# A down projection rewritten from a plain product into seven block products

## The reference, cut to what matters

```python
h = rmsnorm(x, g_norm2) * (1.0 + sc2) + sh2
x = x + gt2 * ((silu(h @ w_gate) * (h @ w_up)) @ w_down)   # w_down: 5632 x 2048, fp32
return rmsnorm(x, g_final)                                 # x: 512 tokens x 2048
```

## Time and profile before

| | |
|---|---|
| median of three runs | 2304.39 us |
| span of the profiled execution, first to last instruction | 2303.3 us |
| TensorE busy in the span | 2249.0 us (98%) |
| VectorE busy | 1532.3 us (67%) |
| ScalarE busy | 887.8 us (39%) |
| GpSimd busy | 233.0 us (10%) |
| mean granted TensorE clock | 0.987 |

### The profile page before, as it was taken

One profiled execution on the slowest core, in us unless ns is written; L12 is line 12 of the kernel. 1 busy time (PEld: TensorE's weight loads), 2 busy tenths in 40 slices (PEclk: granted clock), 3 DMA queues, 4 the chain that ended last, 5 costly groups with the idle time before them and its releaser, 6 DMA issues.

```text
span 2303.3 us, 27075 instructions
## 1 busy us (share of the span) xinstructions
PE 2249.0 (98%) x10486; PEld 1866.6 (81%) x10486; DVE 1532.3 (67%) x1734; ACT 887.8 (39%) x1048; POOL 233.0 (10%) x90
## 2 busy tenths in 40 slices
PE   5999999999999999999999999999999999999998
PEld 5878878888877788788888888888888888888887
DVE  5968667474766757677887788778878544444444
ACT  4333232323246222444444444444444433333333
POOL 0002433333420013000000000000000001010001
PEclk7999999999999999999999999999999999999999
DMA  9943444444541777234444445344434845554553
GB/s 362 377 143 114 166 145 148 150 163 161 183 166 37 275 266 263 92 102 146 155 164 137 145 138 173 128 138 163 160 131 148 326 184 203 193 188 183 192 193 128
DMA packets 188198, 404.43 MB, mean 176 GB/s; under 512 B 11328, under 2 KB 67920, under 8 KB 172496
## 3 DMA queue, kind: packets, MB, share of 16 engines
q1 hardware_dynamic: 175088, 387.10, 47.4%
q10 hardware_dynamic: 13024, 16.13, 2.0%
HBM read 383.27 MB, written 19.92 MB: 175 GB/s over the span
## 4 chain that ended last, share of the span: by engine, by line
PE 90%; DVE 4%; issue 2%; ACT 1%; DMA 1%; POOL 1%; SPq 1%; POOLq 0%; DVEq 0%; ACTq 0%
PE ps L1791 27%; PE ps L1793 27%; PE ps L1792 27%; PE ps L1948 1%; DVE acc L1102 1%; DMA araw<-in_w_ada 1%; PE ps L2235 1%; PE ps L1961 1%; PE ps L1959 1%; DVE acc L1339 1%; PE ps L1882 0%; PE ps L1823 0%; PE ps L2060 0%; PE ps L1937 0%; PE ps L1843 0%
## 5 line engine op out<-in xcount | busy, mean ns | idle before, releaser
L931 ACT ACTIVATE whi<-wraw 128x1024 fp32r<-128x1024 f32 x200 | 211.0, 1061 | 276.5 <-DVE wraw L1614 153.3
L1595 DVE TENSOR_TENSOR wlo<-wraw,whi 128x1024 fp32r<-128x1024 f32 x200 | 240.6, 1219 | 76.8 <-ACT whi L931 76.8
L1791 PE MATMUL ps<-d_hi,whi 128*128 128x512 f32 (+1 forms) x736 | 280.1, 381 | 0.0
L1793 PE MATMUL ps<-d_hi,wlo 128*128 128x512 f32 (+1 forms) x736 | 279.6, 380 | 0.0
L1792 PE MATMUL ps<-d_lo,whi 128*128 128x512 f32 (+1 forms) x736 | 279.6, 380 | 0.0
L1791 PE MATMUL ps<-h_hi,whi 128*128 128x512 f32 x680 | 271.6, 399 | 0.0
L1793 PE MATMUL ps<-h_hi,wlo 128*128 128x512 f32 x680 | 267.0, 393 | 0.0
L1792 PE MATMUL ps<-h_lo,whi 128*128 128x512 f32 x680 | 266.5, 392 | 0.0
L1707 DVE TENSOR_TENSOR d_lo<-d_raw,d_hi 128x2048 fp32r<-128x2048 f32 (+1 forms) x44 | 99.7, 2267 | 243.3 <-ACT d_hi L998 243.3
L1791 PE MATMUL ps<-whi,sk_hi 128*128 128x512 f32 x640 | 250.8, 392 | 0.0
L1793 PE MATMUL ps<-whi,sk_lo 128*128 128x512 f32 x640 | 249.4, 390 | 0.0
(11 more groups left out here) (332 smaller groups left out, 3866.3 us busy)
## 6 DMA issues: line engine op xcount, KB each, us to landing
araw<-in_w_ada SPq DMA_DIRECT2D x64, 1024.0 KB, 6.0
wraw<-in_w_gate SPq DMA_DIRECT2D x88, 512.0 KB, 3.9
wraw<-in_w_up SPq DMA_DIRECT2D x88, 512.0 KB, 4.7
d_raw<-aT_keep SPq DMA_DIRECT2D x44, 1024.0 KB, 4.8
wraw<-in_w_down SPq DMA_DIRECT2D x44, 1024.0 KB, 7.1
wraw<-in_w_in SPq DMA_DIRECT2D x38, 1024.0 KB, 5.3
acc<-in_w_up SPq DMA_DIRECT2D x40, 512.0 KB, 5.5
wraw<-in_w_out SPq DMA_DIRECT2D x16, 1024.0 KB, 8.2
```

The source lines that it names most:

```text
L931: A(EHI[e % 4], src, ACT.Copy).then_inc(uhi_ok, 1)
L1595: V_.tensor_tensor(ELO[e % 4], src, EHI[e % 4].bitcast(F32), ALU.subtract).then_inc(ulo_ok, 1)
L1791: pe.matmul(o, w_hi, m_hi, start=first, stop=False)
L1793: return pe.matmul(o, w_lo, m_hi, start=False, stop=last)
```

## The change

The down projection is cut into blocks: tokens into halves of 256 (a1., a2.), each hidden chunk into halves of 256 rows, and output columns into two groups of 1024 (`n` = 0, 1), each halved into 512. Seven block products replace eight:

| product | block of a | block of w_down | when |
|---|---|---|---|
| P1 | a11 | B11 | early |
| P5 | a21-a22 | B11+B12 | early |
| P6 | a21-a22-a11 | B11+B12+B22 | early |
| P4 | a22 | B11+B12+B22+B21 | early |
| P7 | a11-a21 | B12+B22 | late |
| P2 | a12 | B21 | late |
| P3 | a12+(a21-a22-a11) | B22 | late |

A pass over the 11 chunks does the four early products, a second one the three late ones, and that for both groups: 44 steps (`s`), 154 entries. An entry has 12 matmuls of 512 columns, two 128-token tiles t by two k tiles by three. Now the activations are stationary and the weights move, so the result is tokens x columns, and x1 (not the result) is turned on TensorE (`turn_x1`, 16 x 4 transposes in the late steps of n = 0).

- All seven blocks of a are made per chunk in the unit stage (`combine_a`, four VectorE subtractions or additions of 128x512, each waiting for the one before), and stored in `a_keep` (four rows of 512 per chunk become seven; three more stores on ScalarE's queue per unit, `keep_sums`).
- Of w_down, SyncE loads four pieces of 512 KB in an early step and three in a late one, since the pieces are read again in the late pass. VectorE makes three sums in an early step, one in a late step (`down_sum`, L1913).
- ScalarE makes all high parts (`block_hi`, `down_hi`), VectorE all low parts (`block_lo` L1976, `down_lo` L1902). The entries use the ring of four EHI/ELO buffers of the unit stage.
- The gate gt2 becomes a row (`gain_row`, `gtb`), the squares are summed by ScalarE's accumulation, and GpSimd adds no more squares.
- The two halves of tokens at the end are gone; `take`, `join_x1`, `final_mean` and `scaled_out` end the kernel.

```diff
+        def down_order(s):
+            n, late, j = down_step(s)
+            if late:
+                if s < STEPS - 2:
+                    return [(s, "P7"), (s, "P2"), (s, "P3")]
+                return [(s + i, p) for ps_ in (("P7", "P2"), ("P3",)) for i in range(2) for p in ps_] if s == STEPS - 2 else []
+            if s == 0:
+                return [(0, "P1"), (0, "P5"), (0, "P6")]
+            if s == 1:
+                return [(1, "P1"), (1, "P5"), (0, "P4"), (1, "P6"), (1, "P4")]
...
+        def sums_after(e):
+            due = [(s, name, FIRST_E[s] + i - 2 + (s == 2) + (s == STEPS - 1))
+                   for s in range(STEPS) for i, name in enumerate(("P7",) if down_step(s)[1] else ("P5", "P6", "P4"))]
...
 @block.sync
+            def down_loads(s):
+                if s < 2:
+                    sp.wait_ge(ulo_ok, 28 * NU - 3 + 3 * s)
+                else:
+                    sp.wait_ge(ulo_ok, E0 + END_E[s - 2])
+                for i, (rows, col) in enumerate(((lower, far), (upper, far), (upper, near)) if late else
+                                                ((lower, near), (lower, far), (upper, far), (upper, near))):
+                    sp.dma_start(DRAW[s % 2][i]..., w_down[0, rows, col]...).then_inc(dw_ld[s % 2][i], 16)
...
+            for s in range(STEPS):
+                down_loads(s)
+                if s >= 2:
+                    down_blocks(s)
+                if s == 2:
+                    sp.wait_ge(u_used, 28 * NU)
+                    sp.dma_start(gfb[:], gf.partition_broadcast(P)).then_inc(x_ld[0], 16)
+                    x1_piece(0)
+                    x1_piece(1)
+                if s == NCH + 4:
+                    sp.dma_start(gtb[:], gt_keep...partition_broadcast(P)).then_inc(wg_ld, 16)
+                    x1_piece(2)
+                if s == NCH + 6:
+                    x1_piece(3)
...
 @block.scalar
+            def down_hi(e):
+                s, name = DOWN[e]
+                if e < 4:
+                    act.wait_ge(u_used, 28 * NU - 3 + e)
+                else:
+                    act.wait_ge(u_used, E0 + e - 3)
...
 @block.vector
+            def combine_a(u):
+                V_.tensor_tensor(s3, a11, a21, ALU.subtract).then_inc(ac_ok, 1)
+                dve.wait_ge(ac_ok, 4 * u - 3)
+                V_.tensor_tensor(a21, a21, a22, ALU.subtract).then_inc(ac_ok, 1)
+                dve.wait_ge(ac_ok, 4 * u - 2)
+                V_.tensor_tensor(s2, a21, a11, ALU.subtract).then_inc(ac_ok, 1)
+                dve.wait_ge(ac_ok, 4 * u - 1)
+                V_.tensor_tensor(s4, a12, s2, ALU.add).then_inc(ac_ok, 1)
...
+            for e in range(len(DOWN)):
+                if e == 1:
+                    sum_low(NCH)
+                if e == 2:
                     sum_high(NCH)
+                down_lo(e)
+                if e == 2:
                     sum_up(NCH)
+                if e == 3:
                     join_high(NCH)
+                if e == 4:
                     join_low(NCH)
+                if e == 8:
+                    combine_a(NCH)
+                for s, name in sums_after(e):
+                    down_sum(s, name)
...
+                if e == 2:
+                    block_lo(1)
+                for s in range(2, STEPS):
+                    if e == END_E[s - 2] + 4:
+                        block_lo(s)
...
 @block.tensor
+            def down_entry(e):
+                pe.wait_ge(dal_ok, s + 1)
+                pe.wait_ge(ulo_ok, E0 + e + 1)
+                if j == 0:
+                    pe.wait_ge(*{(0, "P1"): (end_ok, 6 * NCH - 10), (0, "P5"): (end_ok, 6 * NCH - 6), ...
+                for t in range(2):
+                    for k in range(2):
+                        last = mm3(ps[bank + t][:], d_hi[s % 2][:, blk, part], d_lo[s % 2][:, blk, part],
+                                   EHI[e % 4][:, c0], ELO[e % 4][:, c0], j == 0 and k == 0, j == NCH - 1 and k == 1)
```

More of the change, by code:

```diff
@@ L504, in _, with chunk_kept @@
[L504 to L509, removed]
+            def chunk_kept(c):
+                sp.wait_ge(at_st[0], 16 * (c + 1))
+                sp.wait_ge(at_st[1], 32 * (c + 1))
+                sp.wait_ge(as_st, 32 * (c + 1))
+            def down_loads(s):
+                n, late, j = down_step(s)
+                lower, upper = slice(j * S, j * S + HT), slice(j * S + HT, j * S + S)
+                near, far = slice(2 * n * S, 2 * n * S + S), slice(2 * n * S + S, 2 * n * S + 2 * S)
+                if s < 2:
[4 more added lines that the diff above has]
+                                                ((lower, near), (lower, far), (upper, far), (upper, near))):
+                    sp.dma_start(DRAW[s % 2][i].rearrange("p (k c) -> p k c", k=2),
+                                 w_down[0, rows, col].rearrange("(k p) c -> p k c", p=P)).then_inc(dw_ld[s % 2][i], 16)
@@ L510, in _ @@
+            for n, tb in enumerate((2, 3, 0, 1)):
+                for half in range(2):
+                    sp.wait_ge(y_ok[half], n + 1)
+                sp.dma_start(out[0, tb * P:(tb + 1) * P, :], x2[:, tb, :]).then_inc(y_out, 16)
             sp.wait_ge(y_out, 16 * TB)
@@ L569, in _, with final_rs @@
             pool.tensor_tensor(rs, ve, halfneg, ALU.pow).then_inc(n_rs, 1)
[L570 to L580, removed]
+            def final_rs(h):
+                pool.wait_ge(n_ms, 1 + h + 1)
+                two = slice(2 - 2 * h, 4 - 2 * h)
+                pool.tensor_tensor(rs[:, two], ve[:, two], halfneg[:, two], ALU.pow).then_inc(n_rs, 1)
+            final_rs(0)
+            final_rs(1)
         @block.scalar
@@ new lines, in _ @@
+                if e == 2:
+                    block_lo(1)
+                for s in range(2, STEPS):
+                    if e == END_E[s - 2] + 4:
+                        block_lo(s)
+                for i in range(4):
+                    if e == FIRST_E[2 * NCH + 2 + 2 * i]:
+                        join_late(i)
+                    if e == FIRST_E[3 * NCH + 6 + i]:
+                        gain(i)
+            take(0)
+            join_x1(0)
+            take(1)
+            join_x1(1)
+            take(2)
@@ L1787, in _ @@
+            join_x1(2)
+            final_mean(0)
+            for b in range(2):
+                dve.wait_ge(u_used, E0 + end_of(1, "P3") + b)
+                take(3, b)
+                join_x1(3, b)
+            final_mean(1)
+            scaled_out(0)
+            scaled_out(1)
         @block.tensor
```

543 lines of the change are left out of this document (334 added, 209 removed).

## The result

The changed kernel took 2333.66 us (median of 4 runs, 2329.73 to 2336.88) against 2304.18 (4 runs): ratio 1.0122, 95% interval 1.011 to 1.0135. It is slower by 29 us where 22 us less was forecast, and outside the range of 2258 to 2302. The profiled execution has a span of 2335.1 us, 31.8 more than the one before.

What follows compares the result with a forecast made beforehand. The rewritten stage was taken as bound by TensorE's number of matmuls. Work plus waits gave 461.2 us to the last entry, 478.0 with the end against 500.1: span 2281.2, median 2282.3 us, range 2258 to 2302.

Steps and rivals of the forecast that it cites:

- TensorE's part: Down stage: 154 entries, transposes and the gate's row take TensorE 427.1 us without waits.
- The start: Start of the down stage: four waits of TensorE up to step 2, 19.0 us together, the longest 12.4.
- The end: Behind the last entry: final operations and four 1 MB stores take 16.8 us, 5.2 more than before.
- The units: Unit stage: the added block operations on VectorE and the three extra stores cost 0.
- ScalarE ... is no bound: Early steps: ScalarE has 6.2 us of work per step and does not limit the kernel.
- where the sum had 3.0: Early steps of n = 1: VectorE's scale-and-add pairs use up its reserve and lead unevenly, 3.0 us.
- No reserve: I take 0.15 us for each of 20 steps, 3.0: Late steps: VectorE's chain to the blocks' low part takes 5.44 us, as do TensorE's two entries; 3.0 us of waits.
- 5.2: just in time: Late steps: P7's two pieces land 5.2 us after release and are wanted after 5.4.
- the borders, the row of the gate and the last step: Early-to-late changes 2.0 us; gate's row and x1's last pieces in two steps' queue 3.5; last two steps' late blocks 1.5.
- P7's sum waiting for transfers at each late step: Late steps: one of the signs that would show the forecast wrong.
- The rival of late weights: Late steps: weights land too late for the P7 sum, gain gone from 7.8 us on; 2318 us, chance 0.11.
- The clock once, 2.1 us: After the 12 us wait at the stage's start: the clock halves once, costing 2.1 us.

Runs made afterwards that it cites:

- h1: Changed kernel with loads from step 2 on cut to an eighth of the bytes and VectorE's weight sums to 16 columns (output wrong): 2261.5 us.
- f2: Changed kernel with the blocks of a issued ahead of the weight pieces in early steps only: 2319.8 us.
- f4: Changed kernel with only the block loads cut to an eighth of the bytes from step 2 on, weight pieces whole: 2318.0 us.
- f1: Changed kernel with the low part of the blocks of a ahead of the weight sums in VectorE's order: 2313.5 us.
- g1: f3 with each weight piece issued once its own last reader on VectorE is done, not the whole step: 2275.7 us.
- f3: Changed kernel with f1's and f2's edits, and x1 and the final gain's row spread over steps 4, 6 and 8: 2285.4 us.
- g2: g1 with the three weight sums of step 1 one entry later in VectorE's order: 2273.9 us.
- e1: Changed kernel with the blocks of a issued ahead of the weight pieces in all steps: 2352.2 us.
- e3: Changed kernel with weight pieces and block loads cut to an eighth of the bytes from step 2 on: 2275.3 us.

## Why the prediction was wrong

Right: TensorE's part (427.1; h1 about 428). The start (19.0; 19.7), wait by wait, with its cause, though its closeness owes something to luck (above). The end (16.8; 16.9). The units at nothing: TensorE has the same single wait of 1.2 us between 940 us and the stage in both kernels. The last steps' 1.5 (1.4). In the start's burst a 512 KB store of ScalarE's queue took 11.2 us, against 3.2 in the units. By that the trace agrees with the Trainium skill, DMA: Bandwidth & Descriptors, Issuing engines are not separate DMA queues; what the stores cost SyncE's transfers stays open, since no run here took them away.

Wrong, and what the runs show in its place:

1. **A deadline left out.** "ScalarE ... is no bound" looked at its 6.2 us of work, not at when its blocks land. The four pieces and the blocks are one queue, the blocks last; the sum held no term for them. They landed 9 us after their own issue and some 11 after the release, and TensorE waited 15.3 us in the early steps behind step 2, where the sum had 3.0. f2 takes that away alone: 15.3 becomes 1.4, and the kernel is 14 us faster although its late steps wait 6 us more.
2. **"No reserve: I take 0.15 us for each of 20 steps, 3.0", and "5.2: just in time".** The waits of late steps were 24.4 us; the sum had 3.0 for them and 7.0 for the borders, the row of the gate and the last step (of which 2.0, 3.5 and 1.5). Two sizes were off. In the late steps of n = 1 where VectorE waited, the pieces were there 5.5 to 7.0 us after the release, not 5.2 (f4: not for the bytes of the blocks). And VectorE was ready 3.5 to 5.0 us after the release, mostly 4.3, not 5.4, because the low part that releases the pieces was itself late behind the previous blocks: a wait came back in the next step instead of dying out. The sign of being wrong, "P7's sum waiting for transfers at each late step", came in 14 of 22. f1 brings these waits from 24.4 to 12.5 us, g1 brings f3's from 11.4 to 4.7. The rival of late weights (2318, chance 0.11) named the right place, but not the cause: it wanted the pieces to land at 7.8 us or later, and only the two sums beside the gate's row and x1's last pieces started that late (8.1 and 8.4). That its price is near is luck.
3. **The clock once, 2.1 us.** One long wait cost what was estimated (nine matmuls at 0.43 in place of 0.23 us, 1.8 us). But there was one half-clock stretch ahead of it, at the turn of the last chunk, and seven more behind it, each behind a wait of 1.8 to 3.8 us. TensorE's time beyond waits and 427 us of work is 25.4 us in the changed kernel (30 waits, 9 stretches), 6.7 in g2 (11 waits, 2 stretches: 449.2 - 427 - 15.5), 3.3 in h1 (3 and 1). A wait's row also hides 0.16 us: it is counted from the modelled end of a matmul (0.39), where the next would have come after 0.23. How the 25.4 divide is an estimate: at 1.7 us a stretch 15.3 are the clock's, at 0.16 us a wait 4.8 the restarts', and some 5 are left over. A wait's length alone does not decide: one of 1.8 us had a fall behind it, those of 3.2 us at 2144.5 and 2171.4 had none. The Trainium skill's rule, TensorE: Matmul & The Clock Gate, HAM oscillation, that waits for transfers between bursts put the array back to half clock each time, was nearer than my taking it once, though here 30 waits brought 9 stretches and not 30.

```profile
1850.00:1855.00 5.00, 2.90 (x7) 2.33 (x8) 4.31 (x3) 1.30 (x1) 0.00 (x0) 0.50 0.52 199
...
1965.00:1970.00 5.00, 2.30 (x7) 1.88 (x8) 4.92 (x4) 2.70 (x3) 0.00 (x0) 0.86 0.42 164
1970.00:1975.00 5.00, 5.00 (x19) 3.98 (x19) 1.57 (x2) 1.06 (x1) 0.00 (x0) 0.80 0.98 323
...
2145.00:2150.00 5.00, 4.43 (x19) 3.32 (x19) 4.96 (x5) 4.18 (x6) 0.00 (x0) 1.00 0.00 2
```
These rows of the changed kernel are behind the 13.9 us wait, behind one of 3.8 us, and behind one of 3.2 us: in the third, 19 matmuls fit in 5 us where 22 do at 1.00. In the last row the clock stays at 1.00.

So 27 us more of waits (59.4 against 32), 23 more of clock and restarts and the 3 ahead of the stage turn -22 into +32 in the profiled execution, +29 in the median. In the changed kernel as it stands, seven products save some 60 us of TensorE's time; the order of the transfers and of one VectorE operation and the late release of the pieces take them back. g2, with the same operations and bytes, is 30 us faster than the kernel before. What stays open: why the clock falls behind some waits and not behind others, and the longest wait of g2 behind its start (3.0 us at 1984.6, where the gate's row and x1's third piece are in the queue).

## What to carry to other kernels

When a step's engines are filled to nine tenths, busy shares do not tell the time (VectorE at 92% cost TensorE nothing in e1's early steps, and at 80% it cost 20 us by its order in the changed kernel). Write for each tile when it is released, when it lands, and when its in-order reader arrives, for every load of the step and not for the weights alone. Put in each queue, and on each engine, first what the bottleneck needs first; here such moves, without a byte or an operation less, were worth 60 us. And count the clock with the waits, since short ones that come back step by step can cost it again, here seven times in 26.

## What the runs showed of the hardware

- SyncE's issue of a 512 KB transfer took 3.58 us and of a 1 MB one 5.89 us while about 6 MB were in flight (changed kernel), against 0.5 and 0.7 us otherwise.
- The granted clock fell to half behind seven waits of 1.8 to 3.8 us, with TensorE at work before and after, and did not fall behind two of 3.2 us (changed kernel).
- Two 512 KB pieces took 5.4 to 7.1 us from release to use even when the block loads next to them were cut to 96 KB (f4). Their bytes at the 400 GB/s of the burst (396 to 419 in the 5 us windows from 1830 to 1850) are 2.6 us, and a piece of 64 KB takes 2.0 us from issue to landing as well (e3's median over the stage; 4.9 for 512 KB on the page of the changed kernel).
